# Expert tokens in two buffers, a fourth slot list by a 0/1 matrix, and router logits inside the last output tile

## The chip, the cores and the metric

The kernel runs on one core of a Trainium2 chip. A core has five engines that run their own instruction streams and meet at semaphores: TensorE (PE; its weight loads are shown as PEld), VectorE (DVE), ScalarE (ACT), GpSimd (POOL) and SyncE (SP), which here only issues DMAs. Sixteen DMA engines move data between HBM and the on-chip memory. The metric is the device time of one execution in microseconds (us).

## The reference, cut to what matters

One layer of an encoder on 512 tokens of width 1024, in fp32. Three branches (neighbourhood attention, a state-space layer, attention to a memory) are gated and merged; then comes the part that the change touches:

```python
x = x + merged @ w_out[l]
h2 = rms_norm(x, norm_ffn[l])
x = x + hierarchical_moe(h2, ...)
return rms_norm(x, final_norm)

def hierarchical_moe(h, ...):
    coarse = h @ w_coarse + b_coarse                 # 4 groups
    grp = top_k(coarse, 1)                           # one group a token
    fine = (h @ w_fine + b_fine)                     # 4 experts in each group
    top_v, top_i = top_k(fine of the group, 2)       # two experts a token
    w_top = softmax(top_v) * softmax(coarse)[grp]
    ...
    a = silu(h @ w_gate[e]) * (h @ w_up[e]) * comb[e]     # 16 experts, 256 wide
    return sum_e a @ w_down[e]
```

## The kernel before, in words

**Splitting.** A product of fp32 matrices is three products of rounded parts: every operand is stored as hi (rounded to fp32r by ScalarE) and lo (the rest, by VectorE), and TensorE adds hi*hi, lo*hi and hi*lo (lines 1416 to 1418).

**Output tiles.** The 512 tokens are NT = 4 tiles of 128 rows. `out_tile(n)` multiplies tile n of `merged` by w_out in 48 matmuls, the first 24 for columns 0 to 511, the others for 512 to 1023. VectorE adds the product to x (line 1249), ScalarE sums the squares (line 769), and `inverse_root` makes 1/rms. `x2_turn` transposes the new x on TensorE (line 1702), ScalarE and VectorE take it out of PSUM, `logits(n)` multiplies it by the 20 router columns (line 1709). `gffb` holds the norm's gain, h2 the normed tokens. For tile 3 ScalarE scales (line 792), GpSimd multiplies by the gain (line 1981), and GpSimd's queue stores it to `h_scratch`.

**Router.** VectorE turns the logits into choices (from line 1266 on). For experts 0 to NHOT - 1 it makes the list of an expert's tokens at once: 0/1 matrices `hot`, a product with the token numbers on TensorE, and `slot_list` (the semaphore idx0). For the others GpSimd writes tokens and weights to `tok_scratch` with eight indirect DMAs and reads all lists back as `idx`.

**Experts.** Up to CAP = 128 tokens are gathered by GpSimd's indirect DMA from h_scratch into one of three buffers `xg`. `tokens(e)` transposes them (line 1754) into PSUM banks 4 and 5, and ScalarE and VectorE split them into xt_hi and xt_lo (lines 810 and 1350), of which there is one each. An expert's weights are three units of 1 MB: rows 0 to 511 of w_gate and w_up, rows 512 to 1023 of both, and w_down. A unit is two DMAs of 512 KB on SyncE's queue q1 into one of EU = 9 buffers `eraw`; both add to the buffer's semaphore. ScalarE rounds a unit to e_hi, VectorE makes e_lo, in three slots. SyncE loads the next unit into a buffer when VectorE is through with the old one.

**Order in a step e.** TensorE: first half of gate and up of expert e, transpose of act_a of e - 1, second half of e, tokens of e + 1, down product of e - 1. ScalarE scales the down product of e - 1 by the router's weight into `ysb` (line 841), and GpSimd adds it to `acc_scratch` in DRAM with an indirect DMA that reads, adds and writes (line 397). Since two experts may share a token, each such write waits for the one before it. In its loop GpSimd issues for each e the gather of e + 3 and then the write of e - 1. At the end SyncE loads acc_scratch back (line 516), the final norm runs, and the result is stored.

**SyncE's order around the routing.** It loads two units early; four more when the last output tile is done (`out_k`); then it waits for the store of h2, for the logits and for the landing of gather 1 (`xg1`) before it loads the rest, unit by unit.

## Time and profile before

| | us |
|---|---|
| median of 3 runs (lowest, highest) | 735.66 (733.75, 737.59) |
| the profiled execution | 734.23 |
| its span from the first to the last instruction | 732.6 |
| TensorE busy | 643.4 (88%) |
| VectorE, ScalarE, GpSimd busy | 417.0, 333.8, 192.1 |
| rounding of a unit of weights (line 805, ScalarE, mean) | 1.917 |
| rest of a unit of weights (line 1344, VectorE, mean) | 2.288 |

TensorE's share is an average over stages. The routing lies at 505 to 532 us of the span, the experts at 532 to 704, the final norm behind 715. A row of an engine in order of time gives start, length, engine, line, operation, output<-input and shape; in brackets stands how long the engine had been idle and what released it. In the rows of waits stand the total, the number and the longest. The queue q0 carries GpSimd's DMAs, q1 SyncE's.

### The profile page before, as it was taken

What the parts mean: (1) busy time and instruction counts of PE and PEld (TensorE: products, weight loads), DVE (VectorE), ACT (ScalarE), POOL (GpSimd) and SP (SyncE); (2) the same over time, 40 slices, a digit from 0 to 9 for tenths busy, and PEclk for the clock granted to TensorE, in tenths of its full rate; (3) what the DMA queues carried; (4) which work ended last, traced back from release to release, by engine and by line L of the source; (5) the groups of instructions that cost most, each with busy time, mean ns of one, the idle gap of its engine ahead of it and who ended that gap; (6) DMA issues with size and microseconds to landing.
All of it is one profiled execution on the core that took longest, in us unless ns stands there. A gap on an engine that the chain in (4) does not pass through costs nothing.

```text
span 732.6 us, 9196 instructions
## 1 busy us (share of the span) xinstructions
PE 643.4 (88%) x3197; PEld 510.7 (70%) x3197; DVE 417.0 (57%) x783; ACT 333.8 (46%) x565; POOL 192.1 (26%) x191
## 2 busy tenths in 40 slices
PE   2996999989999999999999997999287999999930
PEld 2785888869777766777778785788266877777720
DVE  4988112780475453433652249522866889888814
ACT  4873321221443423434322327322356888888722
POOL 3519921980000000000000000001545424566320
PEclk9999989999999999999999999999588999999975
DMA  9973203221412221111122223624699999999655
GB/s 293 191 166 102 72 30 87 67 78 38 108 58 85 58 58 59 55 33 59 57 83 62 82 89 103 253 110 167 247 349 388 313 340 376 366 357 347 175 87 229
DMA packets 88625, 114.96 MB, mean 157 GB/s; under 512 B 18278, under 2 KB 65480, under 8 KB 88584
## 3 DMA queue, kind: packets, MB, share of 16 engines
q1 hardware_dynamic: 76776, 93.13, 37.8%
q0 software_dynamic: 6848, 18.60, 10.7%
q10 hardware_dynamic: 4960, 2.70, 1.3%
q8 instruction: 24, 0.39, 0.2%
q14 instruction: 17, 0.14, 0.1%
HBM read 102.08 MB, written 15.80 MB: 161 GB/s over the span
## 4 chain that ended last, share of the span: by engine, by line
PE 55%; DMA 19%; DVE 14%; issue 6%; ACT 3%; POOL 2%; SPq 1%; ACTq 0%; DVEq 0%; POOLq 0%
DMA acc_scratch<-ysb,idx 15%; PE bank L1416 13%; PE bank L1418 12%; PE bank L1417 12%; PE bank L1603 3%; PE bank L1575 3%; DVE w_lo L908 2%; PE bank L1592 2%; PE bank L1537 1%; DMA xg<-h_scratch,idx 1%; PE bank L1709 1%; PE bank L1502 1%; POOL tok_scratch L2002 1%; PE bank L1579 1%; ACT w_hi L530 1%
## 5 line engine op out<-in xcount | busy, mean ns | idle before, releaser
L908 DVE TENSOR_TENSOR w_lo<-raw,w_hi 128x1024 fp32r<-128x1024 f32 x55 | 71.3, 1299 | 134.5 <-ACT w_hi L530 134.0
L1416 PE MATMUL bank<-h_hi,w_hi 128*128 128x512 f32 x320 | 133.7, 418 | 3.7 <-DVE w_lo L908 2.4
L1418 PE MATMUL bank<-h_hi,w_lo 128*128 128x512 f32 x320 | 127.3, 398 | 0.0
L1417 PE MATMUL bank<-h_lo,w_hi 128*128 128x512 f32 x320 | 127.1, 397 | 0.0
L1344 DVE TENSOR_TENSOR e_lo<-eraw,e_hi 128x2048 fp32r<-128x2048 f32 x48 | 108.8, 2288 | 18.1 <-ACT e_hi L805 18.1
L805 ACT CAST e_hi<-eraw 128x2048 fp32r<-128x2048 f32 x48 | 91.8, 1917 | 8.9 <-PE bank L1418 5.3
L1955 POOL TENSOR_TENSOR wcf<-wcf,prt 128x160 f32<-128x160 f32 x1 | 0.5, 457 | 308.9 <-DMA wcf<-in_moe_w_fine 308.9
L1416 PEld LDWEIGHTS bank<-h_hi,w_hi 128*128 128x128 f32 x320 | 61.8, 193 | 17.1 <-DVE w_lo L908 2.6
L530 ACT CAST w_hi<-raw 128x1024 fp32r<-128x1024 f32 x55 | 57.6, 1046 | 34.5 <-PE bank L1418 34.5
L1418 PEld LDWEIGHTS bank<-h_hi,w_lo 128*128 128x128 f32 x320 | 61.3, 192 | 13.9
L1417 PEld LDWEIGHTS bank<-h_lo,w_hi 128*128 128x128 f32 x320 | 61.6, 192 | 11.1
L1416 PE MATMUL bank<-e_hi,xt_hi 128*128 128x512 f32 x128 | 53.9, 421 | 7.5 <-DVE xt_lo L1350 7.5
L1418 PE MATMUL bank<-e_hi,xt_lo 128*128 128x512 f32 x128 | 51.2, 400 | 0.0
L1417 PE MATMUL bank<-e_lo,xt_hi 128*128 128x512 f32 x128 | 51.0, 399 | 0.0
L397 POOL DMA_INDIRECT acc_scratch<-ysb,idx x16 | 29.0, 1812 | 81.0 <-DMA acc_scratch<-ysb,idx 56.9
L644 ACT ACTIVATE pr<-ssb,soft 128x192 f32<-128x192 f32 (+1 forms) x32 | 15.4, 482 | 58.2 <-DVE soft L1166 58.2
L1416 PEld LDWEIGHTS bank<-e_hi,xt_hi 128*128 128x128 f32 x128 | 24.7, 193 | 18.0 <-issue 7.8
L632 ACT ACTIVATE gt<-bank,bgh 128x512 f32<-128x512 f32 x24 | 16.5, 688 | 43.0 <-PE bank L1418 43.0
L1987 POOL DMA_INDIRECT xg<-h_scratch,idx x16 | 31.5, 1968 | 9.5 <-DVE idx L1317 6.7
L1161 DVE CUSTOM_DVE_ANT_0 ssb<-bank,ez 128x192 f32<-128x192 f32 (+1 forms) x32 | 12.4, 388 | 30.5 <-PE bank L1575 30.5
L1416 PE MATMUL bank<-e_hi,at_hi 128*128 128x512 f32 x64 | 27.5, 430 | 2.0 <-DVE at_lo L1361 2.0
L1418 PEld LDWEIGHTS bank<-e_hi,xt_lo 128*128 128x128 f32 x128 | 24.6, 192 | 5.6
(377 smaller groups left out, 1312.8 us busy)
## 6 DMA issues: line engine op xcount, KB each, us to landing
raw<-in_w_in SPq DMA_DIRECT2D x40, 512.0 KB, 3.8
eraw<-in_moe_w_gate SPq DMA_DIRECT2D x32, 512.0 KB, 9.1
eraw<-in_moe_w_up SPq DMA_DIRECT2D x32, 512.0 KB, 13.3
eraw<-in_moe_w_down SPq DMA_DIRECT2D x32, 512.0 KB, 10.5
raw<-in_w_out SPq DMA_DIRECT2D x8, 512.0 KB, 3.8
x_sb<-in_x SPq DMA_DIRECT2D x4, 512.0 KB, 5.1
raw<-in_w_mem_kv SPq DMA_DIRECT2D x4, 512.0 KB, 7.5
raw<-in_w_br_na SPq DMA_DIRECT2D x4, 512.0 KB, 3.4
```

Of the source, the lines that this page charges most:

```text
L397: pool.indirect_dma_start(out=acc_dram, out_offset=bass.IndirectOffsetOnAxis(ap=v(idx, 2 * e, [1, 1]), axis=0), in_=v(ysb, D * (e % 2), [1 ...
L530: act.copy(v(dst, o, [1, 1024]), v(raw, 1024 * (c % RAW), [1, 1024])).then_inc(sem("w_hi_done"), 1)
L632: ins = act.activation(v(gt, SEQ * m, [1, SEQ]), pv(g % 2, 0, [1, SEQ]), ACT.Tanh, scale=0.5, bias=v(bgh, KD * branch + m, [1, 1]))
L805: act.copy(v(e_hi[dst], 0, [1, 2048]), v(eraw, 2048 * j, [1, 2048])).then_inc(sem("e_hi_done"), 1)
L908: dve.tensor_tensor(v(l_, o, [1, 1024]), v(raw, 1024 * (c % RAW), [1, 1024]), raw32(v(h_, o, [1, 1024])), SUB).then_inc(sem("w_lo_done"), 1)
L1344: dve.tensor_tensor(v(e_lo[dst], 0, [1, 2048]), v(eraw, 2048 * j, [1, 2048]), raw32(v(e_hi[dst], 0, [1, 2048])), SUB).then_inc(sem("e_lo_d ...
L1416: pe.matmul(dst, w[0], x[0], start=first, stop=False)
L1417: pe.matmul(dst, w[0], x[1], start=False, stop=False)
L1418: return pe.matmul(dst, w[1], x[0], start=False, stop=last)
L1575: pe.matmul(dst, v(qT, SEQ * (h // 2) + P * i, [1, P], p0=lo64, pn=pn), v(kT, SEQ * (h // 2) + w0, [1, n], p0=lo64, pn=pn), start=False, s ...
L1603: ins = pe.matmul(pv(6 + u % 2, 0, [1, HD]), v(pts, 256 * (u % 2) + P * k, [1, P], pn=n), vals, start=k == 0, stop=k == 1)
L1987: pool.indirect_dma_start(out=v(xg, D * (e % 3), [1, D]), out_offset=None, in_=h2_dram, in_offset=bass.IndirectOffsetOnAxis(ap=rows, axis= ...
```

## The change

Three things are changed.

1. xt_hi and xt_lo have two buffers, used by even and odd experts; the second lies where tiles of x_sb were, so its first use waits for `acc_set`. The tokens of e + 1 are transposed on TensorE behind the first half of expert e instead of behind the second, and ScalarE and VectorE split them before the unit 3e + 2 of the weights.
2. NHOT is 4: the list of expert 3 too comes from a 0/1 matrix. Its gather is issued behind the eight writes to tok_scratch, when buffer 0 of xg is free.
3. The last output tile is cut into pieces, with the turn of tile 2, logits 1 and logits 2 between them. Its first half's sum with x, and its squares, are taken half by half. out_k is raised once more, so SyncE's four loads and GpSimd's iotas wait for the value NT + 1. The biased logits of tiles 0 to 2 are made ahead of the last root, those of tile 3 behind it.

```diff
-NHOT = 3
+NHOT = 4
...
-    xt_hi, xt_lo = at("xt_hi", 74.5, KD * P, F32R), at("xt_lo", 78.5, KD * P, F32R)
+    xt_hi = [at(f"xt_hi{j}", kb, KD * P, F32R) for j, kb in enumerate((74.5, 42.5))]
+    xt_lo = [at(f"xt_lo{j}", kb, KD * P, F32R) for j, kb in enumerate((78.5, 46.5))]
...
-        sp.wait_ge(sem("out_k"), NT)
+        sp.wait_ge(sem("out_k"), NT + 1)
         load_unit(0, 1, 2)
...
-        square_x2(NT - 1)
-        x2_take(NT - 1, 0)
-        roots(NT + 3, NT - 1, 1)
+        n = NT - 1
+        for half in range(2):
+            act.wait_ge(sem("x2"), n + half + 1)
+            if half:
+                x2_take(n, 0)
+            ins = act.activation(v(h2, D * n + 512 * half, [1, 512]), v(x_sb, D * n + 512 * half, [1, 512]), ACT.Square,
+                                 accum_out=v(stat, n + half, [1, 1]))
+        ins.then_inc(sem("squares"), 1)
+        roots(n + 4, n, 1)
...
-        def xt_take(e):
+        def xt_take(e, odd):
+            if isinstance(e, int) and e == 1:
+                act.wait_ge(sem("acc_set"), 16 * NT)
+            if not isinstance(e, int) or e >= 2:
+                act.wait_ge(sem("e_used"), 3 * e - 4)
...
             if not peeled or e < 15:
+                xt_take(e + 1, 1 - odd)
                 unit_hi(3 * e + 2, n0 % EU, load_of(n0, i), 2)
...
-                xt_take(e + 1)
                 unit_hi(3 * e + 3, (n0 + 1) % EU, load_of(n0 + 1, i), 0)
...
+        n = NT - 1
+        for half in range(2):
+            dve.wait_ge(sem("out_k"), n + 1 + half)
+            add_x(n, half).then_inc(sem("x2"), 1)
+        dve.wait_ge(sem("x2_turned"), 2 * NT)
+        dve.tensor_copy(v(x2T, SEQ * 4 + P * n, [SEQ, 4], [1, P]), pv(H2_BANK[1], 0, [P, 4], [1, P])).then_inc(
+            sem("x2_last"), 1)
+        dve.wait_ge(sem("lb_in"), 32)
+        for m in range(n):
+            biased(m)
+        dve.wait_ge(sem("squares"), n + 4)
+        link(dve.tensor_tensor(v(stat, n, [1, 1]), v(stat, n, [1, 1]), v(stat, n + 1, [1, 1]), ADD))
+        inverse_root(n + 4, n, 1)
         dve.sem_inc(sem("last_root"), 1)
...
         slot_list(1)
+        one_hot(3)
...
         slot_list(2)
+        slot_list(3)
...
-        out_tile(3)
+        out_tile(3, C_OUT, C_OUT + 4)
         x2_turn(2)
         logits(1)
+        out_tile(3, C_OUT + 4, C_OUT + 6)
         logits(2)
+        out_tile(3, C_OUT + 6, NCH)
         x2_turn(3)
         logits(3)
...
+            if not peeled or e < 15:
+                tokens(e + 1, (e0 + 1) % 3, 16 * (2 * i + (e0 + 1) // 3 + 1))
             if not peeled or e < 16:
                 gate_up(e, 1 if first else 3 * e, 1, 1 if first else 0, odd)
-            if not peeled or e < 15:
-                tokens(e + 1, (e0 + 1) % 3, 16 * (2 * i + (e0 + 1) // 3 + 1))
...
+        pool.wait_ge(sem("idx0"), 4)
+        pool.wait_ge(sem("xt"), 2)
+        gather(3)
         pool.wait_ge(sem("scattered"), 16 * 8)
...
-            if e + 3 < NE:
+            if NHOT <= e + 3 < NE:
                 pool.wait_ge(sem("xt"), 2 * e + 2)
                 gather(e + 3)
```

On TensorE, at the end of the last output tile and behind it, the rows before are these; wp is the last part of w_out, x_sb the new x, wcf the router's columns, and 45 matmuls of the tile stand ahead of the first row:

```order
L1416 MATMUL bank<-wp_hi,m_hi 128x512
L1417 MATMUL bank<-wp_lo,m_hi 128x512
L1418 MATMUL bank<-wp_hi,m_lo 128x512
L1702 MATMUL bank<-ident,x_sb 128x128 x8
L1709 MATMUL bank<-wcf,x2T 128x20 x16
L1702 MATMUL bank<-ident,x_sb 128x128 x8
L1709 MATMUL bank<-wcf,x2T 128x20 x8
L1730 MATMUL bank<-selb,upper 128x64
```

In the changed kernel the turn of tile 2 and logits 1 follow the first half of that tile (wo is the middle part of w_out):

```order
L1440 MATMUL bank<-wo_hi,m_hi 128x512
L1441 MATMUL bank<-wo_lo,m_hi 128x512
L1442 MATMUL bank<-wo_hi,m_lo 128x512
L1727 MATMUL bank<-ident,x_sb 128x128 x8
L1737 MATMUL bank<-wcf,x2T 128x20 x8
L1440 MATMUL bank<-wo_hi,m_hi 128x512
L1441 MATMUL bank<-wo_lo,m_hi 128x512
L1442 MATMUL bank<-wo_hi,m_lo 128x512
```

Logits 2 stand 12 matmuls further on, and only the turn of tile 3 and logits 3 are left behind the tile.

On ScalarE, in steps 0 and 1 of the experts, the rows before, with the semaphores that they wait for:

```order
L805 CAST e_hi_132<-eraw 128x2048 [waits e_in2]
L827 ACTIVATE act_t<-bank 128x256 [waits e_used]
L810 CAST xt_hi<-bank 128x512 [waits xt] x2
L805 CAST e_hi_130<-eraw 128x2048 [waits e_used,e_in3]
L805 CAST e_hi_131<-eraw 128x2048 [waits e_used,e_in4]
L820 CAST at_hi<-bank 128x256 [waits at]
L805 CAST e_hi_132<-eraw 128x2048 [waits e_used,e_in5]
L827 ACTIVATE act_t<-bank 128x256 [waits act_a,e_used]
L810 CAST xt_hi<-bank 128x512 [waits xt] x2
```

and in the changed kernel:

```order
L821 CAST xt_hi_137<-bank 128x512 [waits xt,acc_set]
L821 CAST xt_hi_137<-bank 128x512 [waits xt]
L812 CAST e_hi_132<-eraw 128x2048 [waits e_in2]
L839 ACTIVATE act_t<-bank 128x256 [waits e_used]
L812 CAST e_hi_130<-eraw 128x2048 [waits e_used,e_in3]
L812 CAST e_hi_131<-eraw 128x2048 [waits e_used,e_in4]
L831 CAST at_hi<-bank 128x256 [waits at]
L821 CAST xt_hi_136<-bank 128x512 [waits xt,e_used]
L821 CAST xt_hi_136<-bank 128x512 [waits xt]
L812 CAST e_hi_132<-eraw 128x2048 [waits e_used,e_in5]
L839 ACTIVATE act_t<-bank 128x256 [waits act_a,e_used]
```

The tokens of the next expert (xt_hi) moved from behind the tanh (act_t) to a place ahead of the unit e_hi_132; VectorE's rows moved in the same way.

On GpSimd, behind the routing, the rows before:

```order
L1987 DMA xg<-h_scratch,idx_157 128x1024 [waits idx0,h2_out]
L1987 DMA xg<-h_scratch,idx_157 128x1024 [waits idx0] x2
L1964 DMA acc_scratch<-x_sb 128x1024
L2002 DMA tok_scratch<-pay,rowi 8192x2 [waits tok_zero,iotas,wts,rows]
L2002 DMA tok_scratch<-pay,rowi 8192x2 x7
L2006 DMA idx<-tok_scratch 128x32 [waits scattered]
L2010 COPY wcur<-idx 128x1 [waits idx_in]
L1987 DMA xg<-h_scratch,idx 128x1024 [waits xt]
L2010 COPY wcur<-idx 128x1
```

and in the changed kernel:

```order
L2017 DMA xg<-h_scratch,idx_159 128x1024 [waits idx0,h2_out]
L2017 DMA xg<-h_scratch,idx_159 128x1024 [waits idx0] x2
L1994 DMA acc_scratch<-x_sb 128x1024
L2032 DMA tok_scratch<-pay,rowi 8192x2 [waits tok_zero,iotas,wts,rows]
L2032 DMA tok_scratch<-pay,rowi 8192x2 x7
L2017 DMA xg<-h_scratch,idx_159 128x1024 [waits xt,idx0]
L2039 DMA idx<-tok_scratch 128x32 [waits scattered]
L2043 COPY wcur<-idx 128x1 [waits idx_in]
L2043 COPY wcur<-idx 128x1
```

The gather of expert 3 moved from behind the first wcur to a place ahead of the load of idx.

## Rows read from the trace of the kernel before

**Rows 1.** The page, the chain that ended last: share of the span by line.

```profile
DMA acc_scratch<-ysb,idx 15%; PE bank L1416 13%; PE bank L1418 12%; PE bank L1417 12%; PE bank L1603 3%; PE bank L1575 3%; DVE w_lo L908 2%; PE bank L1592 2%; PE bank L1537 1%; DMA xg<-h_scratch,idx 1%; PE bank L1709 1%; PE bank L1502 1%; POOL tok_scratch L2002 1%; PE bank L1579 1%; ACT w_hi L530 1%
```

**Rows 2.** GpSimd in order of time, 555 to 733 us; last, line 397.

```profile
558.47 3.41 POOL L397 DMA_INDIRECT acc_scratch<-ysb,idx  x1 [0.31 <-issue]
...
572.46 2.36 POOL L397 DMA_INDIRECT acc_scratch<-ysb,idx  x1 [9.15 <-ACT ysb L841]
...
694.83 1.55 POOL L397 DMA_INDIRECT acc_scratch<-ysb,idx  x1 [6.52 <-DMA acc_scratch<-ysb,idx]
...
708.56 1.53 POOL L397 DMA_INDIRECT acc_scratch<-ysb,idx  x1 [5.31 <-DMA acc_scratch<-ysb,idx]
...
DMA to landing us min/median/max: 6.0/9.1/11.8
```

**Rows 3.** DMA queues and issues: first 570 to 580 us, the others 650 to 660.

```profile
eraw<-in_moe_w_up SPq DMA_DIRECT2D x2, 512.0 KB, 7.6
...
q1 hardware_dynamic: 754, 2.74, 68.7%
q0 software_dynamic: 288, 0.86, 34.8%
...
eraw<-in_moe_w_up SPq DMA_DIRECT2D x2, 512.0 KB, 23.4
```

**Rows 4.** ScalarE in order of time, 689 to 706 us.

```profile
689.23 1.91 ACT L805 CAST e_hi<-eraw 128x2048 fp32r<-128x2048 f32 x1 [0.69 <-DMA eraw<-in_moe_w_down]
691.05 1.25 ACT L841 ACTIVATE ysb<-bank,wcur 128x512 f32<-128x512 f32 x2
...
704.18 1.26 ACT L841 ACTIVATE ysb<-bank,wcur 128x512 f32<-128x512 f32 x2 [5.15 <-PE bank L1418]
```

**Rows 5.** TensorE in order of time, 562 to 619 us.

```profile
562.86 1.97 PE L1754 MATMUL bank<-ident,xg 128*128 128x128 f32 x8 [4.29 <-DMA xg<-h_scratch,idx]
...
608.43 0.49 PE L1416 MATMUL bank<-e_hi,xt_hi 128*128 128x512 f32 x1 [0.27 <-DVE xt_lo L1350]
...
618.35 0.49 PE L1416 MATMUL bank<-e_hi,xt_hi 128*128 128x512 f32 x1 [0.28 <-DVE xt_lo L1350]
```

**Rows 6.** Stretch: busy time and count by engine, granted clock, DMA share, GB/s.

```profile
560.00:570.00 10.00, 7.14 (x26) 6.05 (x27) 4.80 (x6) 3.86 (x4) 3.14 (x3) 0.66 1.00 340
```

**Rows 7.** Waits from 440 us on: total us, times, longest.

```profile
PE bank L1416 <- DVE xt_lo L1350: 7.5, 14, 1.7
...
ACT e_hi L805 <- DMA eraw<-in_moe_w_down: 2.5, 2, 1.8
```

**Rows 8.** Routing in order of time, 505 to 553 us; last, h_scratch's stores and gathers.

```profile
505.04 0.33 SPq L466 DMA_DIRECT2D eraw<-in_moe_w_gate  x1
...
505.72 3.65 PE L1709 MATMUL bank<-wcf,x2T 128*128 128x20 f32 x32
...
511.29 0.14 DVE L900 TENSOR_SCALAR stat<-stat 128x1 f32<-128x1 f32 x1
...
512.94 0.16 DVE L341 SCALAR_TENSOR_TENSOR stat<-stat 128x1 f32<-128x1 f32 x1
...
517.06 0.58 POOL L1960 DMA_DIRECT2D h_scratch<-h  x1 [0.30 <-POOL h L1981]
...
523.99 1.10 POOL L1987 DMA_INDIRECT xg<-h_scratch,idx  x1 [6.35 <-DVE idx L1317]
...
530.63 0.33 SPq L466 DMA_DIRECT2D eraw<-in_moe_w_gate  x1
...
547.16 0.59 POOL L2006 DMA_DIRECT2D idx<-tok_scratch  x1 [5.80 <-DMA tok_scratch<-pay,rowi]
...
552.81 2.88 POOL L1987 DMA_INDIRECT xg<-h_scratch,idx  x1 [0.56 <-issue]
...
DMA to landing us min/median/max: 2.9/3.0/6.0
...
DMA to landing us min/median/max: 4.5/9.3/10.0
```

More of the change, by code:

```diff
@@ L1259, in _, with add_x @@
[L1259 to L1267 removed]
+        def add_x(n, half):
+            xs = v(x_sb, D * n + 512 * half, [1, 512])
+            return dve.tensor_tensor(xs, pv(2 * (n % 2) + half, 0, [1, 512]), xs, ADD)
@@ new lines, in biased @@
+        def biased(n):
+            dve.wait_ge(sem("logits"), n + 1)
+            return dve.scalar_tensor_tensor(v(rt, 20 * n, [1, 20]), pv(5 + n // 3, 20 * n, [1, 20]), v(stat, 24 + n, [1, 1]),
+                                            v(lbias, 0, [1, 20]), MUL, ADD)
+        for n in range(NT - 1):
+            dve.wait_ge(sem("out_k"), n + 1)
+            add_x(n, 0)
+            add_x(n, 1).then_inc(sem("x2"), 1)
+            inverse_root(n + 4, n, 1)
+            dve.scalar_tensor_tensor(v(h2, D * n, [1, D]), v(x_sb, D * n, [1, D]), v(stat, 24 + n, [1, 1]),
+                                     v(gffb, 0, [1, D]), MUL, MUL).then_inc(sem("h2"), 1)
@@ L1676, in _, with out_tile @@
                 s5_outputs()
-        def out_tile(n):
-            for c in range(C_OUT, NCH):
+        def out_tile(n, c0=C_OUT, c1=NCH):
+            for c in range(c0, c1):
                 half, kp = divmod(c - C_OUT, 4)
@@ L1991, in _ @@
         pool.wait_ge(sem("h2_out"), 16 * NT)
-        for e in range(NHOT):
+        for e in range(3):
             pool.wait_ge(sem("idx0"), e + 1)
```

58 lines of the change are left out of this document (23 added, 35 removed).

## The prediction

> **What bounds the kernel now.** The page comes first. Its chain of work that ended last [rows 1] gives 15% of the span to one kind of transfer, the accumulating write acc_scratch<-ysb, more than to any line of TensorE. I then read GpSimd's instructions in order of time from 550 us on [rows 2]. Expert 0's write is issued at 558.47 us, expert 1's at 572.46, expert 13's at 694.83 and expert 15's, the last, at 708.56. Each waits for the one before to land. One lands in 6.0 us at the least and 9.1 us in the median, so between 572 and 709 us there is never room between two of them. The reader is to see a serial chain that is longer than TensorE's own work.
>
> The second reading asks what that chain competes with. The DMA queues from 650 to 660 us [rows 3] show the weight queue q1 moving 2.74 MB beside 0.86 MB on GpSimd's queue q0, the two together at 103.5% of 16 engines. An expert's weights are 6 transfers of 512 KB, 3.15 MB. TensorE passes an expert in 9.92 us, from 608.43 to 618.35 [rows 5], so it eats 3.17 MB in 10 us and is given 2.74. The difference comes out of the nine buffers of eraw, and the landing times tell how much is left: w_up is the second transfer on its buffer's semaphore, so its landing says when the whole unit is in, and that is 7.6 us after its issue at 570 to 580 us and 23.4 us after it at 650 to 660. While 8 experts were consumed (80 us) the supply fell behind by 23.4 - 7.6 = 15.8 us, so 8 experts' weights take 95.8 us, about 12 us an expert. At the end it shows: ScalarE's rounding of a unit of w_down waits for its landing at 689.23 us, and expert 13's output stands behind it at 691.05 [rows 4]. So the last weights land when the DMA engines have moved them, whatever TensorE does in the middle. They were saturated from the moment the second batch of loads was let go (530.63 us) [rows 8].
>
> **What the change takes away on TensorE.** (a) Expert 3's tokens: TensorE stands still 4.3 us before 562.86 [rows 5], since the list of expert 3 comes back over tok_scratch and its gather is issued at 552.81 only. The granted clock then stands at its lower level, 1.2 GHz, for a while: its mean from 560 to 570 us is 0.66 [rows 6], so 3.4 us of work at 2.4 GHz are lost in it, less about 1 us that fell into idle time: 2.4 us. With the fourth list made by the 0/1 matrix the gather is issued right behind the eight writes to tok_scratch, ahead of the wait for their landing, which begins at 547.16 - 5.80 = 541.4 [rows 8]; with the start below, near 543. Even at 10 us it lands by 553, ahead of the 555 to 558 us at which TensorE now asks for it. Gone: 4.3 + 2.4 = 6.7 us. (b) The waits for xt_lo: 7.5 us in 14 [rows 7], 0.27 to 0.28 us in the middle steps [rows 5], and about 0.07 for the restart. With two buffers a step costs 9.92 - 0.35 = 9.57 us. TensorE's side would be 6.7 + 10 x 0.35 = about 10 us ahead at the end, less the start below.
>
> Not everything there is gain. In step 0 ScalarE and VectorE now take expert 1's tokens before the third weight unit, and these tokens are there only after half of expert 0. The unit (1.9 us on ScalarE, 2.3 on VectorE by the table of the profile) then comes last, and TensorE starts expert 1 about 0.5 us later than before relative to its start. This lies ahead of the gain (a) and I take 0.5 out of it. The new waits (acc_set before the first use of buffer 1, e_used later) name things that are done 1 to 2 us sooner; behind them on ScalarE stand the roundings of weights, for which VectorE and TensorE wait, so a late acc_set would cost its whole lateness. I cost them at 0.
>
> **What the change adds at the start.** Logits 1 and 2 (32 instructions, 3.65 us) and the turn of tile 2 (about 0.87 us) move from behind the output tile into it [rows 8]. The tile therefore ends at 505.0 (SyncE's loads, which wait for it, are issued at 505.04) + 4.5 = 509.5. SyncE's four units, 4.2 MB, go to 509.6 and land as much later. Behind the tile VectorE has the second half's add (0.65), the turn (0.65) and the copy (0.7), ending at 511.7 instead of 511.4; then three biased rows (0.5) and the sum of the two halves (0.2) stand ahead of the root. The root took 1.8 us, from 511.29 to 513.10. It will end at 511.7 + 0.7 + 1.8 = 514.2, so 1.1 us later. Only one biased row is left behind it instead of a wait for logits 3 and four rows, so the router's comparisons start about 1 us sooner. That gains nothing: the first gather at 523.99 waits for two things, its list and the store of h2's last tile, issued at 517.06 and landed 6.0 us later, at 523.1 [rows 8]. The store is behind the root, over ScalarE's scaling and GpSimd's multiply, and takes the root's 1.1 us along. It moves to 518.1, lands at 524.2, now beside loads that end near 525 and not 520.5. The extra one_hot and slot_list (0.86 + 0.5 us on VectorE) eat what the router gained before weights 0 and 1 are split. So gathers 0 and 1 go about 1.1 us later, 1.3 with the loads' tail, and the landing of gather 1 is what lets SyncE issue the second batch: 530.63 becomes 531.9. Bounds for this term: -1, if the list, which comes about 1 us sooner, and not the store decides; +5.3, if gather 1, which took 5.1 us on idle DMA engines, meets the loads and takes the 9.3 us of the loaded median [rows 8], on top of the 1.1. I take +1.3, near the lower end, since the loads end before the gather's packets start.
>
> **The sum.** The last weights: +1.3 from the start, and +0.5 because the accumulating writes run ahead and more of q0's work is done before them. So the last units land 1.8 us later, and expert 13's output, scaled by ScalarE from 691.05 to 692.3, is ready at 694.1. Against that, the chain of writes loses its own lag. Its second write moved from 572.46 to where the first, issued at about 557.5 and landed 11 us later, lets it go: 569. It then stays 3.5 us ahead, expert 12's write lands by 693.4, and expert 13's write starts at its own output, 694.1 + 0.3 = 694.4, instead of 694.83: -0.4. Behind it stand three writes of 6.1 us with 0.75 between them and the unchanged finish. Expert 15's output (704.18 + 1.26 + 1.8 = 707.2) is ready before the chain reaches it at 708.2. Sum: -0.4 us on the span of 732.6. The profiled execution took 734.23 us and would take 733.8; the median of the runs shown is 1.4 us above it, so I say 735.3 us. Of 10 us taken from TensorE nothing arrives: from about expert 9 on it waits for weights.
>
> **Rivals.** 1. *The loads aren't the bound.* For it: ScalarE's two waits for w_down come to 2.5 us in the whole trace [rows 7]. Against it: landing times that grow without a break. Then the writes start 3.5 us ahead, the loads end some 10 us sooner, and more of the writes take 6.9 us a piece, not 9.8: about 735.7 - 10.5 = 725 us. The Trainium skill (DMA: Bandwidth & Descriptors, section Bandwidth) stands on this side: it measured 425 GB/s for one large transfer, far over the 3.60 MB in 10 us here, so by its rule there is slack and the time is this rival's. Rows 3 do not agree: the engines are busy 103.5% of the time at 360 GB/s, and that carries the forecast. 2. *In between:* the supply gives way in part, for instance because the gathers and writes fall differently beside it, and the chain of writes is what stays, 3.5 us ahead: 732.2 us. 3. *The start is worse (the slower side).* The four units, 4.6 us later, collide with h2's store and gathers 0 and 1. With 9 us for the store and 9.3 for gather 1 the second batch goes 1.1 + 3 + 4.2 = 8.3 us later. All saturated transfers shift by that, so 735.7 - 2.2 + 0.5 + 8.3 = 742 us. It decides from a shift of 5.5 us on. For it: under load the median gather takes 9.3 us; against it, GpSimd's issue comes after the loads are through. 4. *The fourth list is no sooner,* because its gather queues behind the eight writes of tok_scratch (up to 7 us to land): TensorE waits as before, the end is set by the loads, 736 us.
>
> **Chances.** Forecast 0.55 (own range 732.5 to 738.5); rival 1, 0.13; rival 2, 0.15; rival 3, 0.12; rival 4, 0.05. Repeated runs of this kernel differ by about 0.5%, 3.7 us, and this is the bound for no change: 732.0 to 739.3. Faster: rival 1, a little under half of rival 2, a little of the forecast, 0.25. Slower: rival 3 and the upper tail, 0.13. Same: 0.62. The range leaves out rival 1 and the worst of rival 3: 728 to 740.
>
> **What would show it.** Right: GpSimd issues gather 3 before the idx load, near 543, and TensorE's 4.3 us wait at 562 is gone; no waits for xt_lo from step 2 on; SyncE's batches at 509.6 and 532; TensorE starts expert 3 about 5 us earlier; ScalarE's waits for w_down grow from 2.5 to over 6 us; w_up landings at 20 us or more; expert 13's write near 694.5. Wrong: the last eraw landing before 688 us (rival 1 or 2), gather 1 landing after 535 (rival 3), or xg still waited for in step 2 (rival 4).

## The result and the profile after

The changed kernel takes 740.21 us (median, 737.74 to 743.16), against 734.47 for the kernel before (731.04 to 737.59) in the same session. The ratio is 1.0082 (95% interval 1.0061 to 1.0104), so the change costs 0.8%. The profiled execution took 742.04 us with a span of 740.4, 7.8 us more than before.

The first view is the page's chain that ended last. Where [rows 1] gave the accumulating write 15%, it now has 20%, by far its largest entry, and 5% of 740 us is more than the whole loss.

```profile
DMA acc_scratch<-ysb,idx 20%; PE bank L1440 14%; PE bank L1442 12%; PE bank L1441 12%; PE bank L1627 3%; PE bank L1599 2%; DVE w_lo L919 2%; PE bank L1616 2%; PE bank L1561 1%; PE bank L1526 1%; DMA h_scratch<-h 1%; PE bank L1603 1%; DVE m_lo L1197 1%; ACT w_hi L531 1%; PE bank L1537 1%
```

Next, GpSimd in order of time in the changed kernel. The rows are the writes of experts 0, 7, 8, 12, 13 and 15. They answer to [rows 2].

```profile
560.29 2.63 POOL L398 DMA_INDIRECT acc_scratch<-ysb,idx  x1 [2.69 <-PE bank L1784]
...
636.12 3.08 POOL L398 DMA_INDIRECT acc_scratch<-ysb,idx  x1 [6.83 <-DMA acc_scratch<-ysb,idx]
...
647.85 2.48 POOL L398 DMA_INDIRECT acc_scratch<-ysb,idx  x1 [5.25 <-DMA acc_scratch<-ysb,idx]
...
693.23 2.81 POOL L398 DMA_INDIRECT acc_scratch<-ysb,idx  x1 [8.09 <-DMA acc_scratch<-ysb,idx]
...
701.40 2.30 POOL L398 DMA_INDIRECT acc_scratch<-ysb,idx  x1 [3.76 <-DMA acc_scratch<-ysb,idx]
...
716.62 1.53 POOL L398 DMA_INDIRECT acc_scratch<-ysb,idx  x1 [5.40 <-DMA acc_scratch<-ysb,idx]
...
DMA to landing us min/median/max: 6.0/10.0/11.5
```

The write of expert 7 is still 0.9 us ahead of before (there 637.01); that of expert 8 is 0.9 us behind (there 646.95), that of expert 12 7.0 us behind (686.21) and the last 8.06. From expert 2's on, each write waits for the landing of the one before, and the median landing took 10.0 us where it took 9.1. The reader is to look at the second column, how long GpSimd spends on issuing a write. It is 1.5 us at the end and 2.0 to 3.1 from expert 5's write to expert 13's; in the kernel before it was 1.6 us for experts 5 to 11. In the grouped view of lines the 16 issues stand together, first before, then after (busy time in sum, mean ns, idle time ahead of them and its releasers):

```profile
L397 POOL DMA_INDIRECT acc_scratch<-ysb,idx x16 | 29.0, 1812 | 81.0 <-DMA acc_scratch<-ysb,idx 56.9 <-PE bank L1754 14.6 <-ACT ysb L841 9.2
```

```profile
L398 POOL DMA_INDIRECT acc_scratch<-ysb,idx x16 | 36.9, 2309 | 96.2 <-DMA acc_scratch<-ysb,idx 86.2 <-issue 7.3 <-PE bank L1784 2.7
```

The issues grew by 7.9 us. The 16 times from issue to landing, added up row by row, grew from 142.55 to 150.60 us, by 8.05. So nearly all of the landings' growth lies in their first part, the issue. That the last write also starts 8.06 us later is a coincidence of numbers: 1.8 us of it were there at the first write (560.29 against 558.47), and the chain from the first write to the last is 6.2 us longer, less than the landings grew, since some gaps between writes became shorter.

GpSimd did not get slower as a whole. Its 16 gathers show the reverse, before and after:

```profile
L1987 POOL DMA_INDIRECT xg<-h_scratch,idx x16 | 31.5, 1968 | 9.5 <-DVE idx L1317 6.7 <-issue 2.8
```

```profile
L2017 POOL DMA_INDIRECT xg<-h_scratch,idx x16 | 24.3, 1521 | 10.8 <-DMA h_scratch<-h 8.0 <-issue 2.9
```

Gathers and writes together took 60.5 us of issuing before and 61.2 after. The long issues moved from the gathers to the writes, which are the ones in the chain.

What lengthens an issue is seen by laying VectorE beside it. In the changed kernel, VectorE in order of time around the issue at 636.12:

```profile
634.66 0.41 DVE L1393 SCALAR_TENSOR_TENSOR act_s<-act_t,bank 128x256 f32<-128x256 f32 x1
635.11 0.42 DVE L1396 SCALAR_TENSOR_TENSOR act_a<-act_s,bank 128x256 f32<-128x256 f32 x1
635.45 2.28 DVE L1368 TENSOR_TENSOR e_lo<-eraw,e_hi 128x2048 fp32r<-128x2048 f32 x1
```

The subtraction ends at 637.73, and the issue at 636.12 + 3.08 = 639.20, 1.47 us behind it. In the kernel before, GpSimd and VectorE around the issue at 646.95:

```profile
646.95 1.59 POOL L397 DMA_INDIRECT acc_scratch<-ysb,idx  x1 [3.48 <-DMA acc_scratch<-ysb,idx]
```

```profile
646.43 0.42 DVE L1371 SCALAR_TENSOR_TENSOR act_a<-act_s,bank 128x256 f32<-128x256 f32 x1
646.76 1.28 DVE L1350 TENSOR_TENSOR xt_lo<-bank,xt_hi 128x512 fp32r<-128x512 f32 x2
647.96 4.48 DVE L1344 TENSOR_TENSOR e_lo<-eraw,e_hi 128x2048 fp32r<-128x2048 f32 x2
```

Here the write was issued beside the rests of the tokens, which VectorE reads from PSUM, and the issue took 1.59 us; the next e_lo began 1.01 us behind the issue's start. The change moved these rests ahead of act_a, and e_lo now stands right behind act_a.

The start, in order of time in the changed kernel, answers to [rows 8]:

```profile
509.26 0.33 SPq L467 DMA_DIRECT2D eraw<-in_moe_w_gate  x1
...
517.72 0.58 POOL L1990 DMA_DIRECT2D h_scratch<-h  x1 [0.30 <-POOL h L2011]
...
526.26 1.10 POOL L2017 DMA_INDIRECT xg<-h_scratch,idx  x1 [7.96 <-DMA h_scratch<-h]
...
533.53 0.33 SPq L467 DMA_DIRECT2D eraw<-in_moe_w_gate  x1
...
542.90 1.06 POOL L2017 DMA_INDIRECT xg<-h_scratch,idx  x1 [0.30 <-issue]
```

h2's store is issued 0.7 us later but lands 7.65 us after that (at 525.37), not 6.0. Gather 0 is 2.3 us later and the second batch 2.9. Gather 3 is issued at 542.90 and lands at 553.49. TensorE no longer waits for it. It waits instead for e_lo before expert 1, and the granted clock is low in another stretch than in [rows 6]; the second row of windows answers to that one:

```profile
545.69 0.47 PE L1440 MATMUL bank<-e_hi,xt_hi 128*128 128x512 f32 x1 [2.27 <-DVE e_lo L1368]
```

```profile
545.00:555.00 10.00, 9.31 (x39) 7.62 (x40) 8.49 (x9) 6.53 (x8) 0.58 (x1) 0.83 0.98 349
560.00:570.00 10.00, 10.00 (x54) 8.51 (x53) 9.65 (x9) 9.09 (x12) 3.90 (x3) 1.00 1.03 354
```

The length of a step is read from ScalarE's tanh, one per expert:

```profile
600.70 0.39 ACT L839 ACTIVATE act_t<-bank 128x256 f32<-128x256 f32 x1 [0.31 <-PE bank L1442]
610.01 0.39 ACT L839 ACTIVATE act_t<-bank 128x256 f32<-128x256 f32 x1 [0.31 <-PE bank L1442]
620.96 0.42 ACT L839 ACTIVATE act_t<-bank 128x256 f32<-128x256 f32 x1
632.29 0.42 ACT L839 ACTIVATE act_t<-bank 128x256 f32<-128x256 f32 x1
643.42 0.42 ACT L839 ACTIVATE act_t<-bank 128x256 f32<-128x256 f32 x1
```

Up to 610 us a step takes 9.31 us, less than before (9.92). Then it takes 11.0 to 11.7, and in most of these steps ScalarE stands still for about 3 us until w_down has landed. Its waits for w_down [rows 7] grew to 20.6 us:

```profile
ACT e_hi L812 <- DMA eraw<-in_moe_w_down: 20.6, 7, 3.5
```

So weights bound the steps from 610 us on, and the chain follows the outputs at a distance. The last weights land 4.1 us later than before (227.2 against 223.1 us, counted from the first residual add, VectorE's sum of x and the output tile), the last write starts 8.4 us later from the same point. ScalarE in order of time, the outputs of experts 12, 13 and 15, answers to [rows 4]:

```profile
684.98 1.26 ACT L852 ACTIVATE ysb<-bank,wcur 128x512 f32<-128x512 f32 x2
...
695.17 1.26 ACT L852 ACTIVATE ysb<-bank,wcur 128x512 f32<-128x512 f32 x2
...
709.01 1.26 ACT L852 ACTIVATE ysb<-bank,wcur 128x512 f32<-128x512 f32 x2 [6.42 <-DMA acc_scratch<-ysb,idx]
```

Expert 12's output is ready at 686.2 and its write issued at 693.23, 7 us later; before, that distance was 3.9 us. Expert 13's output comes 4.1 us later than before (691.05), its write 6.6. ScalarE stands still for 6.4 us before expert 15's output, and the row names the chain, which holds the buffer of ysb. But TensorE's last matmul of that product ends at 707.73 only:

```profile
707.33 0.40 PE L1442 MATMUL bank<-e_hi,at_lo 128*128 128x512 f32 x1
```

So the buffer costs 1.3 us of the 6.4, and without the chain the output would still have come 3.5 us later than the 704.18 of before. Its write starts at 716.62, 6.3 us behind the output's end at 710.27; before, the last write stood 3.1 us behind its output (705.44, 708.56).

### The profile page after: what moved, and what is told of

Read it like the earlier page. It is cut to its first block, busy times and chain, and to the rows that moved or that the text cites. A ratio compares the mean times of both kernels' runs of the same rounds, so it can differ in the third digit from the quotient of the medians.

```text
span 740.4 us, 9223 instructions
## 1 busy us (share of the span) xinstructions
PE 642.4 (87%) x3201; PEld 508.2 (69%) x3201; DVE 420.2 (57%) x791; ACT 331.2 (45%) x567; POOL 182.1 (25%) x191
## 4 chain that ended last, share of the span: by engine, by line
PE 55%; DMA 24%; DVE 12%; issue 4%; ACT 3%; SPq 1%; ACTq 0%; POOL 0%; DVEq 0%; POOLq 0%
DMA acc_scratch<-ysb,idx 20%; PE bank L1440 14%; PE bank L1442 12%; PE bank L1441 12%; PE bank L1627 3%; PE bank L1599 2%; DVE w_lo L919 2%; PE bank L1616 2%; PE bank L1561 1%; PE bank L1526 1%; DMA h_scratch<-h 1%; PE bank L1603 1%; DVE m_lo L1197 1%; ACT w_hi L531 1%; PE bank L1537 1%
## 5 line engine op out<-in xcount | busy, mean ns | idle before, releaser
L1368 DVE TENSOR_TENSOR e_lo<-eraw,e_hi 128x2048 fp32r<-128x2048 f32 x48 | 109.2, 2290 | 21.2 <-ACT e_hi L812 21.2
L812 ACT CAST e_hi<-eraw 128x2048 fp32r<-128x2048 f32 x48 | 92.0, 1920 | 27.2 <-DMA eraw<-in_moe_w_down 20.6
L398 POOL DMA_INDIRECT acc_scratch<-ysb,idx x16 | 36.9, 2309 | 96.2 <-DMA acc_scratch<-ysb,idx 86.2
L1441 PEld LDWEIGHTS bank<-e_lo,xt_hi 128*128 128x128 f32 x128 | 25.0, 195 | 4.6
```

What stands on the lines that cost most here:

```text
L398: pool.indirect_dma_start(out=acc_dram, out_offset=bass.IndirectOffsetOnAxis(ap=v(idx, 2 * e, [1, 1]), axis=0), in_=v(ysb, D * (e % 2), [1 ...
L812: act.copy(v(e_hi[dst], 0, [1, 2048]), v(eraw, 2048 * j, [1, 2048])).then_inc(sem("e_hi_done"), 1)
L1368: dve.tensor_tensor(v(e_lo[dst], 0, [1, 2048]), v(eraw, 2048 * j, [1, 2048]), raw32(v(e_hi[dst], 0, [1, 2048])), SUB).then_inc(sem("e_lo_d ...
L1441: pe.matmul(dst, w[0], x[1], start=False, stop=False)
```

## The experiments

Theory L (lock): a write that GpSimd issues while an e_lo subtraction runs on VectorE is issued only when that has ended; the new order of VectorE makes this the rule, the chain of writes gets longer than anything beside it, and the rest follows. Rival D: the DMA engines' loads set the end, and the new start delays them. The table has every run, each ratio against the kernel before in the same session (its medians there were 734.47 to 735.23 us); "issues" is the sum of the grouped view as above, "chain" the time from the first write's issue to the last's, both of the one profiled execution.

| kernel | median us | ratio to before (95%) | issues | chain |
|---|---|---|---|---|
| before | 734.47 | | 29.0 | 150.1 |
| changed | 740.21 | 1.0082 (1.0061 to 1.0104) | 36.9 | 156.3 |
| rest_behind | 748.28 | 1.0193 (1.0153 to 1.0232) | 31.0 | 159.9 |
| split_four | 737.12 | 1.0034 (1.0007 to 1.0060) | 29.9 | 152.9 |
| split_two | 737.37 | 1.0023 (0.9997 to 1.0048) | 29.4 | 151.7 |
| turn_behind | 738.28 | 1.0065 (1.0032 to 1.0098) | 32.4 | 151.8 |
| buffers_only | 740.15 | 1.0058 (1.0022 to 1.0095) | 36.4 | 157.6 |
| start_only | 739.46 | 1.0045 (1.0016 to 1.0073) | 27.9 | 152.3 |
| list_only | 735.85 | 0.9996 (0.9965 to 1.0026) | 28.3 | 151.2 |
| old_start | 736.65 | 1.0027 (0.9995 to 1.0060) | 36.0 | 153.6 |
| three_units | 740.89 | 1.0063 (1.0037 to 1.0088) | 37.8 | 156.6 |
| step0_old | 742.17 | 1.0077 (1.0052 to 1.0102) | 31.0 | 153.4 |
| no_xg1 | 747.44 | 1.0182 (1.0134 to 1.0230) | 37.6 | 153.1 |
| before_split | 734.07 | 0.9979 (0.9952 to 1.0006) | 28.2 | 153.6 |
| list_split | 733.73 | 0.9988 (0.9955 to 1.0020) | 31.1 | 153.2 |
| old_start_split | 733.25 | 0.9976 (0.9951 to 1.0000) | 29.9 | 151.7 |
| the same again | 733.68 | 0.9973 (0.9951 to 0.9995) | 29.9 | 149.8 |
| two_chains | 734.76 | 0.9991 (0.9962 to 1.0020) | 40.3 | 148.6 |
| before_two_chains | 734.55 | 0.9992 (0.9966 to 1.0019) | 39.2 | 149.8 |
| old_start_two_chains | 730.39 | 0.9934 (0.9911 to 0.9956) | 39.4 | 146.1 |

**The parts alone.** Each is the kernel before with one part of the diff shown above.

```diff
 buffers_only: xt_hi, xt_lo in two buffers, xt_take/xt_rest/tokens a unit sooner
 start_only:   out_tile in pieces with logits between, halves of x2, out_k NT + 1
 list_only:    NHOT = 4, HOT_BANK, one_hot(3), slot_list(3), gather(3) ahead of the wait for scattered
```

> The kernel before with two buffers for the turned tokens and the sooner turn alone (old start, three lists). Theory L: TensorE's step in the unloaded part goes from 9.9 to 9.3 us, and the writes' issue falls onto running e_lo subtractions: 16 issues of 34 to 37 us against 29.0, which costs 5 to 8 us of the chain, less the slack of 2.7 us and the earlier start of TensorE: 736 to 740 us. If the sooner turn is a gain that the start hides: 731 to 734 us.

> The kernel before with the new start alone (logits of tiles 0 to 2 inside the last output tile, the tile's last half seen by its own semaphore, one buffer, three lists). Theory start: TensorE's tile ends 4.5 us later, SyncE's four units are issued and land 4.5 us later and run beside the store of h2's last tile, which takes 7.6 us instead of 6.0; gather 1 lands 3 us later and with it the second batch. Then everything behind moves by 2.5 to 3.5 us: 737.5 to 738.5 us. What the prediction had (1.3 us): 736.3. If the start costs nothing by itself: 735.

> The kernel before with the fourth slot list alone (old start, one buffer, old order of the turn). TensorE's 4.3 us wait for expert 3's tokens goes; VectorE's order in the steps stays that of before, so by theory L the issues stay near 29 us together and nothing is lost: 732 to 735 us, the lower end if the second accumulating write comes earlier. By the prediction's step (saturated loads set the end) nothing is gained either: 735. If the fourth list is what brings the kernel out of its good phase, the issues grow to 34 us or more and the time to 738 or more.

Two parts cost and the third gives nothing: 0.58%, 0.45% and -0.04%, which add up to 0.99% where all three cost 0.82%. The buffers alone bring the long issues (36.4 us); GpSimd in order of time shows them from 590 us on:

```profile
591.77 3.23 POOL L398 DMA_INDIRECT acc_scratch<-ysb,idx  x1 [6.27 <-DMA acc_scratch<-ysb,idx]
...
603.70 3.60 POOL L398 DMA_INDIRECT acc_scratch<-ysb,idx  x1 [4.04 <-DMA acc_scratch<-ysb,idx]
...
616.30 2.50 POOL L398 DMA_INDIRECT acc_scratch<-ysb,idx  x1 [7.01 <-DMA acc_scratch<-ysb,idx]
```

start_only and list_only keep VectorE's old order and have 27.9 and 28.3 us. The fourth list's chain was 4.9 us ahead of before at expert 5's write (counted from the first residual add), and 1.6 behind at the last: the gain was taken back, as the prediction had it for the middle.

**The start undone.**

```diff
-        sp.wait_ge(sem("out_k"), NT + 1)
+        sp.wait_ge(sem("out_k"), NT)
 ... and every other line of start_only back as before
```

> The changed kernel with the start undone: logits behind the last output tile, SyncE's four units at the tile's old end, one semaphore for the tile. Two buffers, the sooner turn and the fourth list stay. Rival D expects the whole loss to go: second batch of loads at 530.6 instead of 533.5, last weights 3 to 4 us sooner, 736 or, with TensorE's gains, less. Theory L: the first write starts about 2 us sooner, which is worth at most 2 us; the issues of the middle stay at 2.5 to 3 us: 737 to 740 us.

0.55% less than the changed kernel, 4.0 us by the ratios. The median, 736.65 us, lies between L's range (737 to 740) and D's 736, so the time does not tell them apart. The issues stay at 36.0 us, as L said, and the chain is still 3.5 us longer than before.

**The lock: shorter subtractions.**

```diff
-            dve.tensor_tensor(v(e_lo[dst], 0, [1, 2048]), ...
+            for c in range(0, 2048, 512):          # split_two: 1024
+                ins = dve.tensor_tensor(v(e_lo[dst], c, [1, 512]), ...
```

> The changed kernel, with each e_lo subtraction of 2048 columns cut into four of 512 (about 0.63 us each, some 0.2 us more in sum). Theory L: GpSimd gets its turn between two pieces, so no issue of a write takes over about 2.3 us and the 16 together 26 to 31 us instead of 36.9: 733 to 736 us, although VectorE has more to do. Rival D: no gain, 740 to 742 us (VectorE's work grows by some 0.3 us per unit in 48 units, most of it hidden). If the pieces follow so closely that GpSimd gets no turn between them, the issues stay at 36 us or grow, and the time is 740 or more; then L is not refuted by it.

> The changed kernel with each e_lo cut into two of 1024 columns (1.2 us each). Theory L: a piece blocks GpSimd half as long as the whole and twice as long as a quarter, so the 16 issues sum to between 29.9 (four pieces) and 36.9 us (whole), near 32 to 33, and the time lies between 737.1 and 740.2: 738 to 739 us. If the gain of four pieces was something else, such as results coming sooner, there is no such order.

Both shorten the issues as L says and give back 3.1 and 2.8 us, by ratios 0.48 and 0.59%, with more instructions on VectorE. That two pieces do as well as four was not expected. The median issue is 1.64 to 1.65 us in both, and the longest is longer with four (3.8 us). That issue, from 590.25 to 594.06 us, began beside the first of four pieces, which follow each other without a gap until 592.60 and end 1.46 us ahead of it: GpSimd got no turn between them.

```profile
L398 POOL DMA_INDIRECT acc_scratch<-ysb,idx x16: 1534/1641/2567, 562.1 to 713.7; - x16
```

```profile
L398 POOL DMA_INDIRECT acc_scratch<-ysb,idx x16: 1534/1646/3811, 558.3 to 711.2; - x16
```

(minimum/median/maximum in ns, first and last start; split_two, then split_four.)

> The kernel before (median 735.0 us), with each e_lo subtraction of 2048 columns cut into four of 512. In its steady part from 617 to 686 us the writes' issue already falls between two e_lo (1.59 us each), so theory L has little to give: the 16 issues 29.0 us become 27 to 30, and the time 732 to 736 us. If cutting the subtraction gains as much here as in the changed kernel (3.1 us), then its gain is not the lock on the write's issue but something else (VectorE's results coming sooner, or shorter waits of the gathers).

On the kernel before the same edit gives 0.21%, with an interval that holds no change. With the runs below the comparison gets firmer. In kernels with the new order of the turn, cutting e_lo gave 0.48 (four pieces), 0.59 (two), and 0.51 and 0.54% (old_start_split, measured twice, against old_start). In kernels with the old order it gave 0.21 (before_split) and 0.08% (list_split against list_only). The larger part of the gain thus hangs on the new order, as L says. Up to 0.2% may be something else, and single intervals are as wide as that.

**The order of the turn.**

```diff
 rest_behind, VectorE alone:
-                xt_rest(e + 1, 1 - odd)
                 unit_lo(3 * e + 2, n0 % EU, 2)
 ...
+                xt_rest(e + 1, 1 - odd)
                 unit_lo(3 * e + 3, (n0 + 1) % EU, 0)
 turn_behind: that, and the same for xt_take on ScalarE and tokens on TensorE
```

> The changed kernel (median 740.2 us), with one thing moved: VectorE takes the rests of the next expert's turned tokens (xt_rest, two operations of 0.65 us from PSUM) behind act_a again, as before, and not ahead of the third weight unit. ScalarE and TensorE keep the new order. Theory L (lock): the slowdown is GpSimd's issue of the accumulating writes, which takes 1.55 us, or, where an e_lo subtraction (2.3 us) is already running on VectorE, until 1.5 us behind its end; the 16 issues together took 29.0 us before and 36.9 us after, 7.9 us of the 8.1 by which the 16 landings grew. In the old order no e_lo stands right behind act_a, where the write's issue fell in the steady part of before. Then the issues come back to 29 to 32 us together and the kernel takes 733 to 736 us. Rival D (loads): the end is set by the DMA engines, whose last weights land 3.7 us later than before; VectorE's order changes nothing of that: 739 to 741 us, issues at 36 us or shorter with no gain. Rival P (phase is chance): the issues fall anywhere against e_lo: 735 to 743.

> The changed kernel with the turn at its old place on all three engines (TensorE behind the second half of gate and up, ScalarE and VectorE behind act_a), but with two buffers, the fourth list and the new start. Theory L: VectorE's order is that of before, so issues of 29 to 32 us together, and 733 to 737 us, less the 2 us that the start costs at most. Rival D: 740 us. A third view (the sooner turn is what makes TensorE faster, 9.31 us a step against 9.92): steps of 9.5 to 9.9 us.

rest_behind refutes the time that L gave for it: the issues fell to 31.0 us as foreseen, and the kernel became 8 us slower than the changed one. Its steps take 11.05 us (tanh at 600.81, 611.86, 622.93), and TensorE waits in each of them, here the row of its waits from 600 to 690 us:

```profile
PE bank L1440 <- DVE xt_lo L1374: 11.7, 8, 1.5
```

With the tokens turned early on TensorE but their rests late on VectorE, a loop closes: rests (1.3 us), first half of gate and up, transposes of act_a, turn of the tokens, second half, tanh, act_s, act_a, rests again. I had looked at the lock and not at this loop. turn_behind, without that flaw, has issues of 32.4 us and a chain 4.6 us shorter than the changed kernel's, but its ratio of 1.0065 lies within the changed kernel's interval, and its 738.28 us lies above the 733 to 737 that L gave. Its steps up to expert 8 are 9.9 us again, so it also gives up what the sooner turn gains. The order alone brings back less than cutting the subtractions does, and short issues alone don't make the kernel fast.

**Which wait of the start.**

```diff
 three_units: load_unit(0, 2, 5) behind sp.wait_ge(sem("xg1"), 16)
 no_xg1:      sp.wait_ge(sem("xg1"), 16) removed
 step0_old:   in step 0, unit_hi(2) and unit_lo(2) ahead of xt_take(1) and xt_rest(1)
```

> The changed kernel (740.2 us) with one of SyncE's four units (1 MB) behind the landing of gather 1 and not ahead of it. If the start costs because these loads, issued 4.5 us later, run beside h2's store and the first gathers: the store lands in 6.0 to 6.5 us instead of 7.6, gather 0 is issued 1.2 to 1.6 us sooner and the second batch with it: 1 to 2.5 us less, 738 to 739. If the total of the bytes sets the end, the unit's own delay takes it back: 740 to 742.

> The changed kernel, but in step 0 ScalarE and VectorE take the third weight unit ahead of expert 1's tokens, as before. In the profile TensorE waits 2.3 us for that unit before expert 1 and unit 11 is loaded 8.7 us later than before. If that delay counts, 1.5 to 3 us less: 737 to 738.5; if DMA and the chain of writes hide it: 739.5 to 740.5.

> The changed kernel without SyncE's wait for gather 1: the second batch of loads goes as soon as h2's store has landed, 7.5 us sooner, and runs beside gathers 0 to 2. Start by bytes (idle DMA engines between the batches are the loss): 736 to 738 us. Start by the gathers (they take 9 us each under load, expert 0 begins 4 us later and the first write with it): 741 to 744 us.

With three units h2's store landed in 6.66 us instead of 7.65 and the second batch went 0.7 us sooner, counted from the first residual add, but the first write was issued no sooner: no gain. Undoing the order of step 0 gained nothing either (742.17 us, where 739.5 to 740.5 was expected if it didn't count). This run too has short issues, 31.0 us, and a chain 3.0 us shorter than the changed kernel's; in its profile the first write comes 1.9 us later from the first residual add, and the time did not fall. With turn_behind it is the second kernel in which shorter issues brought no time, and L doesn't explain it.

Without the wait for gather 1 the second batch goes 8.2 us sooner, and the kernel is 7 us slower, beyond both ranges that were expected (736 to 738 and 741 to 744), since TensorE gets its first tokens later. The row is TensorE's turn of expert 0's tokens:

```profile
532.96 1.94 PE L1783 MATMUL bank<-ident,xg 128*128 128x128 f32 x8 [11.01 <-DMA xg<-h_scratch,idx]
```

Its first matmul of expert 0 is 4.3 us and its first write 7.4 us later than the changed kernel's, from the first residual add, and the median time 7.2 us longer. In the profile only 4.2 us of the 7.4 are left at the last write, and the profiled execution, with 744.18 us, was faster than the median, so how much of such a delay reaches the end isn't settled.

**The chain taken apart.**

```diff
+        chain, base = (("y_acc", 0), ("scattered", 16 * 8))[e % 2]
-            pool.wait_ge(sem("y_acc"), 16 * e)
+            pool.wait_ge(sem(chain), base + 16 * (e // 2))
-        pool.indirect_dma_start(out=acc_dram,
+        pool.indirect_dma_start(out=(acc_dram, acc2_dram)[e % 2],
```

> The changed kernel with two accumulators: the outputs of odd experts are added into a second one in DRAM, so a write waits for the write before the last and not for the last. Left out: the second accumulator isn't zeroed and not added at the end, so the time has no cost of these. If the serial chain of writes carries the loss (theory L): the writes follow TensorE's outputs, the steps behind 610 us come back from 11.3 to under 10.5 us, and the time falls by 8 us or more, under 732 us. If the loads carry it (the prediction's step): the last unit lands at 227 us behind the first residual add as now, expert 15's output follows it by some 15 us, and only the last two waits of 6.9 us go: 734 to 737 us.

> The kernel before with the same two accumulators and the same work left out. Here TensorE's step of 9.9 us and the chain's 9.85 us are alike, so taking the chain apart gains little in the middle and up to 4 us at the end, where expert 15's output was ready near 707 and its write was issued at 708.56: 729 to 734 us. If the changed kernel's order is better once the chain is gone, two_chains comes out below this one by some us; if the loads bound both, they come out alike up to the start's 3.6 us.

> The changed kernel with the start undone and two accumulators (the second not zeroed and not added at the end: left out). If the loads are the floor of two_chains (734.8) the sooner second batch shows at the end: 731 to 732.5 us. If TensorE and the last outputs are the floor and the loads keep up: also 731 to 732.5, but ScalarE's waits for the landings of w_up and w_down, 20.9 us in two_chains, fall under 12. If the start's loss went only through the chain: 734 to 735 us.

The changed kernel gains 0.91% (6.7 us), the kernel before nothing that shows (0.9992). ScalarE's wait for a buffer of ysb goes by the two chains as well. In two_chains the issues are even longer, 40.3 us, and the writes land in a median of 10.3, but they wait for ScalarE's ysb and no longer for each other:

```profile
L400 POOL DMA_INDIRECT acc_scratch<-ysb,idx x16 | 40.3, 2519 | 89.9 <-ACT ysb L856 62.2 <-PE bank L1788 27.7
```

So the issue counts only where the chain is serial. Without the serial chain the changed kernel is as fast as the kernel before, so its net loss needs the chain; the kernel before was not bound by it alone. Two parts of L's expectation failed. The time, 734.76 us, is not under 732 but in the range that D gave (734 to 737), and the steps behind 610 us did not come back to 10.5 us. ScalarE's tanh in two_chains stands at 611.07, 623.62, 633.51, 646.00 and 656.89, 11.5 us apart in the mean, so these steps are set by the weights with the chain or without it. What goes is the distance between the outputs and their writes. With the chain gone and the old start the kernel takes 730.39 us, 4.4 less than two_chains, so there the start costs as much as anywhere else: its cost doesn't need the chain, and in two_chains it only cancels what buffers and list gain. The last weights land 223.5 us behind the first residual add, against 230.7 in two_chains. ScalarE's waits for w_up and w_down are 18.9 us against 20.9, not under 12, so both still wait for weights.

**The best version.** It cuts e_lo into four pieces in old_start.

> The changed kernel with the start undone and e_lo cut into four of 512: the two causes together. If they add up (start 3.6 us by old_start, lock 3.1 us by split_four, from 740.2 us): 733.5 us, and the best version so far. If the two are one thing (the loads' delay puts the writes into a worse phase): 736 to 737 us as each alone.

> The same kernel as old_start_split (changed kernel, old start, e_lo in four pieces), measured again on another occasion: 733.25 us and 0.9976 of before the first time. If it is truly better: 0.994 to 0.998 again. If that was chance: 0.999 to 1.002.

The two causes add up, and the version is 0.24 and 0.27% faster than before, the second time with an interval below 1. Against list_split the buffers make no difference that shows:

> The kernel before with the fourth slot list and e_lo cut into four of 512: old start, one buffer, old order of the turn. Each alone came out at no difference (0.9996 and 0.9979 of before). If they add up: 733.5 us. It stands against the best so far, old_start_split at 0.9976 of before; if it is as fast, the two buffers bring nothing even where the lock is eased.

The two-chain kernels leave work out, so their time isn't one of a finished kernel. A version that zeroes and adds the second accumulator was not tried, and whether its 0.66% survives stays open.

## Why the prediction was wrong

**What held.** Gather 3 was foreseen near 543 (542.90) and landing by 553 (553.49). The wait for it, the low clock at 560 to 570 us and the waits for xt_lo in the middle are gone. The loads were saturated, and the kernel before was not bound by the chain alone: taking it apart gave 0.9992.

**The step that failed** is the sentence "it then stays 3.5 us ahead". I took the chain's links from [rows 2], as landings of 9.1 us in the median, and let the rest of the chain keep its durations. The second write came at 571.64 and not at 569, and expert 3's was still 3.2 us ahead of before (592.37 against 595.61). From there to expert 11's write a landing took 9.8 to 11.5 us. Expert 13's write was due at 694.4 and came at 701.40: 2.3 of the 7.0 us because its output was ready at 696.43 and not at 694.1, the other 4.7 because the chain was still behind it. The cause is the part of each link that GpSimd spends on the issue: 36.9 us in sum, not 29.0. The rows that could have warned stood in [rows 2]: three writes of 1.53 to 1.55 us, but one of 3.41 and one of 2.36, the same instruction at the same size. I never asked what stretched them. The forecast treated the end as the later of two sides, loads and chain, and had the chain 3.5 us ahead; it was 7 us behind expert 12's output (3.9 in the kernel before) when the last weights came.

The Trainium skill has a mechanism of this kind (SBUF — State Buffer, section 🔬 SBUF: two separate sides): GpSimd writes the descriptors of its DMAs itself, and while VectorE runs an operation in a two-port mode and so holds the port pair that the two share, it can't, so that the DMA seems slow. By the same section an operation with two SBUF inputs takes the pair only against a GpSimd operation that reads SBUF, and whichever engine starts first keeps the pair for its whole instruction while the other waits. This case's traces agree on the wait, with 1.59 us for an issue beside operations that read PSUM, and 3.08 us for one that met a subtraction of two SBUF operands. They don't agree that either side waits: a subtraction that met a running issue took its usual 2.29 us. That the port pair is the reason, no run here shows.

**The start** was mis-sized, at 1.3 us for the second batch (measured: 2.9 in the pair of profiles; in time 3.3 us by start_only, 4.0 by old_start, 4.4 with the chain taken apart). The last weights were due 1.8 us later and landed 4.1 us later. The root came only 0.7 us later, not 1.1, but the store, which I kept at 6.0 us, took 7.65 beside the loads: of the two pieces of rival 3 (store 9 us, gather 1 9.3 us) half of the first came true. The rival gave 742 us, close to the result, by a shift of 8.3 us that did not happen, so its nearness is luck. Sending the second batch sooner is no remedy: no_xg1 had it 8.2 us earlier than the changed kernel, and its last unit landed only 0.6 us earlier, since later units wait for buffers that a late TensorE frees late. That 2.9 us at the second batch cost 3.3 to 4.4 us in time is no riddle once all profiles are read: counted from the first residual add, the second batch goes at 64.9 to 68.6 us in the eight traces with the new start unaltered and at 61.8 to 63.6 in the ten with the old one, 3.7 us apart in the mean. The pair before and changed was a mild case. The store took 7.5 to 8.1 us in the eight and 5.9 to 6.5 in the ten.

**The step** was mis-sized too, on the good side. TensorE came to 9.31 us and not 9.57. **Step 0** was priced at 0.5 us. The profile shows expert 1 3.0 us later than before (545.69 against 542.72), of which 2.05 us were there at expert 0's first matmul (534.07 against 532.02), so step 0 itself took 0.9 us; undoing its order in step0_old gained nothing. With the start, this left TensorE 2.0 us ahead at expert 3's tanh (572.78 against 574.76), where the prediction had expert 3 about 5 us earlier.

**Why the gain of 10 us on TensorE does not arrive.** The prediction said that it waits for weights. That is so, but not all: with the chain taken apart and the old start, buffers and list bring 0.9934 against 0.9992, some 4.3 us. In the changed kernel the lock took about 3.5 us (by split_four) and the start 3.3 to 4.0. With both undone (old_start_split) 1.8 to 2.0 us of a gain are left, so the three add up to the loss of 6.0 us only roughly.

## What to carry to other kernels

A serial chain of DMAs from GpSimd is as long as its issues and its transfers together, and an issue's length depends on what VectorE runs beside it. Where one instruction shows 1.5 us in one row and 3 in another, find what ran beside it before moving anything on VectorE; an edit that leaves both engines' work the same can shift one onto the other. Cutting the long two-operand subtraction in two raised VectorE's busy time on them from 109.2 to 112.5 us, left 2.57 us as the longest issue, and gave back more than half of the loss. And an early turn must be early on all of its engines, or it closes a loop.

## What the runs showed of the hardware

In the 14 traces with whole e_lo subtractions 132 writes were issued while one had been running for at least 0.1 us. Every one of these issues ended 1.43 to 1.53 us behind the subtraction's end. Of the 92 others 90 took 1.53 to 1.64 us; the other two met an e_lo that had begun 0.08 and 0.09 us ahead and took 3.6 and 3.7. Three that met one begun 0.01 to 0.02 us ahead took 1.57 to 1.59. When GpSimd was first, by as little as 0.06 us (581.75 against 581.81 in the changed kernel), its issue took 1.59 us, and the subtraction wasn't lengthened either: it took 2.29 us there, and 2.276 to 2.383 in all its occurrences in the 14 traces. So in this pair only GpSimd pays.

Of a write's landing, what is left behind the issue was 4.5 to 4.6 us for the last two, behind the last loads, and 7.4 to 10.2 for experts 0 to 11, in the kernel before and the changed one. The time of the first residual add varied from 463.3 to 470.7 us between the profiled executions of kernels whose work up to there is the same, so single spans were compared from that point on.
